# Masked scores of two heads in one bank: TensorE adds the mask, VectorE takes both minima at once, ScalarE exponentiates from PSUM

## What is computed

```python
def blk(i):                       # forgetting_attention, one block of 128 queries
    mask = pos[None, :] <= tq[:, None]
    s = jnp.einsum('bqhd,bshd->bhqs', qb, kf) + cq[..., None] - c[:, :, None, :]
    p = jax.nn.softmax(jnp.where(mask, s, -jnp.inf), axis=-1)
    return jnp.einsum('bhqs,bshd->bqhd', p, vf)
```

## Time and profile before

| | |
|---|---|
| median of 3 runs | 1352.73 us (1351.6 to 1353.11) |
| profiled execution | 1355.96 us, span 1354.3 us |
| TensorE busy, mean granted clock | 1330.4 us (98%), 0.993 |
| VectorE busy | 641.7 us (47%) |
| ScalarE busy | 243.1 us (18%) |
| units 16 to 47 with what is between (a0) | 107.69 to 150.92 us |
| units 48 to 79 with what is between (a1) | 460.38 to 497.84 us |

### The profile page before, as it was taken

The page is one execution under the profiler, slowest core; times in us unless marked ns, Lnnn a source line. Parts: engine busy times, 40 slices in busy tenths (PEclk is TensorE's granted clock), DMA queues, the critical chain, the costliest instruction groups (busy, mean ns, idle before and its releaser), DMA issues.

```text
span 1354.3 us, 18984 instructions
## 1 busy us (share of the span) xinstructions
PE 1330.4 (98%) x7306; PEld 823.3 (61%) x7306; DVE 641.7 (47%) x1224; ACT 243.1 (18%) x573; POOL 89.1 (7%) x114
## 2 busy tenths in 40 slices
PE   9999999999999999999999999999999999999996
PEld 8677575786747856586686675744444444444433
DVE  1226589877862257977979263421221222212213
ACT  2135311211102450120123162100000000000002
POOL 1116500000000120000000100000000000000001
PEclk9997999999999999999999999999999999999999
DMA  9931154565453414676574405399999999999994
GB/s 381 354 109 65 64 205 178 219 237 216 183 197 150 157 45 190 236 292 263 221 276 168 158 34 216 147 421 419 421 421 413 422 421 421 422 420 421 421 421 195
DMA packets 51006, 359.53 MB, mean 265 GB/s; under 512 B 5888, under 2 KB 6096, under 8 KB 8432
## 3 DMA queue, kind: packets, MB, share of 16 engines
q1 hardware_dynamic: 45248, 324.60, 59.5%
q0 software_dynamic: 5392, 32.05, 6.6%
q10 hardware_dynamic: 288, 1.80, 0.3%
HBM read 356.88 MB, written 1.05 MB: 264 GB/s over the span
## 4 chain that ended last, share of the span: by engine, by line
PE 82%; DVE 7%; issue 1%; ACT 1%; DVEq 0%; ACTq 0%
PE ps L1470 13%; PE ps L980 13%; PE ps L971 11%; PE ps L1499 7%; PE ps L1395 7%; PE ps L1448 7%; PE ps L953 5%; PE ps L794 4%; PE ps L799 2%; PE ps L873 2%; PE ps L892 1%; PE ps L831 1%; PE ps L1355 1%; PE ps L1224 1%; PE ps L1241 1%
## 5 line engine op out<-in xcount | busy, mean ns | idle before, releaser
L2698 DVE TENSOR_TENSOR masked_and_probs<-ps,gate_rows 128x512 f32<-128x512 f32 x52 | 33.5, 686 | 152.4 <-PE ps L1499 152.4
L794 PE MATMUL ps<-xT,ring 128*128 128x256 f32 x432 | 94.7, 380 | 0.8 <-DVE xT L1992 0.8
L1448 PE MATMUL ps<-masked_and_probs,probT 128*128 128x512 f32 x208 | 94.4, 594 | 1.0 <-DVE masked_and_probs L2698 1.0
L1395 PE MATMUL ps<-masked_and_probs,mix_rows 128*128 128x256 f32 (+1 forms) x416 | 93.0, 376 | 0.0
L1395 PEld LDWEIGHTS ps<-masked_and_probs,mix_rows 128*128 128x128 f32 x416 | 75.0, 190 | 28.8 <-issue 19.6
L971 PEld LDWEIGHTS ps<-xT,ring 128*128 128x128 f32 x768 | 87.8, 192 | 3.8 <-issue 3.8
L1607 ACT ACTIVATE qk_tiles<-ps 64x256 f32<-64x256 f32 (+3 forms) x84 | 39.2, 468 | 278.0 <-PE ps L971 241.8
L794 PEld LDWEIGHTS ps<-xT,ring 128*128 128x128 f32 x432 | 81.5, 190 | 12.3 <-ACT xT L1595 1.0
L971 PE MATMUL ps<-xT,ring 128*128 128x128 f32 x768 | 88.7, 275 | 0.0
L980 PE MATMUL ps<-ring,qk_tiles 128*128 128x512 f32 x192 | 85.2, 592 | 0.0
L953 PE MATMUL ps<-ring,xT 128*128 128x512 f32 x192 | 83.8, 593 | 0.0
(11 more groups left out here) (469 smaller groups left out, 2260.8 us busy)
## 6 DMA issues: line engine op xcount, KB each, us to landing
ring<-in_stream SPq DMA_DIRECT2D x200, 1024.0 KB, 8.6
qk_tiles<-in_stream SPq DMA_DIRECT2D x46, 1024.0 KB, 20.3
v_rows<-in_ada POOLq DMA_DIRECT2D x12, 1024.0 KB, 5.1
qk_tiles<-in_ada POOLq DMA_DIRECT2D x12, 1024.0 KB, 5.2
vec_rows<-in_stream SPq DMA_DIRECT2D x12, 1024.0 KB, 17.2
con<-in_stream SPq DMA_DIRECT2D x12, 1024.0 KB, 18.2
y_rows<-in_stream SPq DMA_DIRECT2D x12, 1024.0 KB, 19.7
par<-in_stream SPq DMA_DIRECT2D x12, 1024.0 KB, 20.8
```

The costliest lines, as they stand in the source:

```text
L794: mm = pe.matmul(ps[0:n, bank, off:off + T], w[:, kk, col:col + n], src[:, k, :], start=bank not in started, stop=k == KT - 1, skip_group_ ...
L1395: mm = pe.matmul(ps[:, 5 + kk // 2, kk % 2 * 2 * P:kk % 2 * 2 * P + width], h2[:, t, k * P:(k + 1) * P], select[:, t, 0:width], start=t == ...
L1448: mm = pe.matmul(ps[:, q, :], probT[:, buf, 256 + q // 2 * P:256 + (q // 2 + 1) * P], yslot[:, q % 2 * 512:(q % 2 + 1) * 512], start=False ...
L2698: dve.tensor_tensor(yslot[:, cols], ps[:, 5 + half, :], gaterow[:, 1, cols], ALU.mult).then_inc(ready, 1)
```

## The change

In units 16 to 79 (`PAIRED`) two heads go through the stages together.

- TensorE writes the scores of both into one bank, side by side, and after each adds the mask on the diagonal block of 128 keys: the product of the identity and `hidden`, which is the negated causal mask, accumulated onto the scores (L899 and L902 of the kernel after, in `masked_scores`). Scale and sign have moved into ScalarE's copies of keys and queries.
- VectorE takes the minima of both heads with one TENSOR_REDUCE from PSUM (L2239) and copies both transposed heads with one COPY (L2264). `masked` is no longer written.
- ScalarE's exponentials read the bank. It copies no transposed heads in a1 any more, and makes `hidden` once (128x128).
- The scores of a pair wait for the exponentials of an earlier pair (`s_exp`) and no longer for `s_mask`: up to unit 35 for the pair two before, then for the pair four before.
- The transposes of a pair come at step i-4, the values at i-6, in a0 and a1.
- In the second kind the order of heads is 0, 2, 1, 3, 4, 6, 5, 7, so that both heads of a pair lie in the same 64 partitions. `sum_column` keeps the columns of `esum` in the old order.
- Units 34 and 35 still use two banks (`TWO_BANKS`), and a0 has one step more.

```diff
+PAIRED = range(16, 80)
-            for h in range(8):
+            for h in (0, 2, 1, 3, 4, 6, 5, 7):
-TWO_BANKS = 34
+TWO_BANKS = 36
 def by_scalar(u):
-    return u % 4 == 1 and (UNITS[u][0] == "loc" or ...)
+    return u % 4 == 1 and u not in PAIRED and (UNITS[u][0] == "loc" or ...)
+        hidden = causal[:, 0, P:2 * P]
+        def pair_scores(u):
+            p, nk = u // 2, UNITS[u][3]
+            bank = p % 2 if u < TWO_BANKS else (0, 1, 6, 7)[p % 4]
+            return ps[:, bank, 0:2 * nk].rearrange("p (n k) -> p n k", n=2)
...
+            def wait_scores_read(u):
+                if u < INSTANCES["a0"][1]:
+                    if u == PAIRED[0]:
+                        pe.wait_ge(s_mask, u)
+                    elif u > PAIRED[0] + 2:
+                        pe.wait_ge(s_exp, u - 2 if u < TWO_BANKS else u - 6)
+                elif u >= INSTANCES["a1"][0] + 8:
+                    pe.wait_ge(s_exp, u - 6)
+            def masked_scores(u, pair):
+                def mask(n):
+                    qt, nk = UNITS[u + n][1], UNITS[u + n][3]
+                    return pe.matmul(scores(u + n)[:, qt * P:nk], ident, hidden, start=False, stop=True, skip_group_check=True)
+                for n, (lhs, keys) in enumerate(pair):
+                    pe.matmul(scores(u + n), lhs, keys[0][0], start=True, stop=False, skip_group_check=True)
+                    mm = mask(n)
+                mm.then_inc(s_sc, 2)
+            def turn_pair(u):
+                pe.wait_ge(s_exp, u + 2)
+                if u == PAIRED[0] and u < INSTANCES["a1"][0]:
+                    pe.wait_ge(s_pTsb, u - 1)
+                elif u >= PAIRED[0] + 2:
+                    pe.wait_ge(s_pTsb, u - 2)
+                for n in range(2):
+                    for t in range(UNITS[u][3] // P):
+                        mm = pe.transpose(turned_bank(u + n)[:, t * P:(t + 1) * P], prob[:, (u + n) % 4, t * P:(t + 1) * P], ident)
+                mm.then_inc(s_pT, 2)
...
+                    u = i - 4
+                    if a <= u < b and u in PAIRED and u % 2 == 0:
+                        turn_pair(u)
...
+                    u = i - 6
+                    if name == "a0" and a <= u < b and u in PAIRED and u % 2 == 0:
+                        row_sums(u)
+                        row_sums(u + 1)
...
-                        act.activation(prob[:, u % 4, 0:nk], masked[:, u % 4, 0:nk], ACT.Exp, bias=negmax[:, u:u + 1],
-                                       scale=-1.0, accum_out=esum[:, u:u + 1]).then_inc(s_exp, 1)
+                        act.activation(prob[:, u % 4, 0:nk], scores(u) if u in PAIRED else masked[:, u % 4, 0:nk], ACT.Exp, bias=negmax[:, u:u + 1],
+                                       scale=-1.0, accum_out=esum[:, sum_column(u):sum_column(u) + 1]).then_inc(s_exp, 1)
+            copy(hidden, causal[:, 0, 0:P], scale=-1.0)
-            copy(kvraw[:, 0, :], ps[:, 1, 0:T])
+            copy(kvraw[:, 0, :], ps[:, 1, 0:T], scale=-SCALE)
...
+                    if i < b and i in PAIRED and i % 2 == 0:
+                        dve.wait_ge(s_sc, i + 2)
+                        dve.tensor_reduce(negmax[:, i:i + 2], pair_scores(i), AX, ALU.min).then_inc(s_mask, 2)
...
+                    u = i - 4
+                    if a <= u < b and u in PAIRED and u % 2 == 0:
+                        dve.wait_ge(s_pT, u + 2)
+                        dve.tensor_copy(pair_probs(u), pair_turned(u)).then_inc(s_pTsb, 2)
```

More of the change, by code:

```diff
@@ L236, with sum_column @@
 ROPE_AT = (12, 16)
+PAIRED = range(16, 80)
 def by_scalar(u):
-    return u % 4 == 1 and (UNITS[u][0] == "loc" or UNITS[u][0] == "fox" and UNITS[u][1] == 1)
+    return u % 4 == 1 and u not in PAIRED and (UNITS[u][0] == "loc" or UNITS[u][0] == "fox" and UNITS[u][1] == 1)
 def taken_before(u, scalar):
     return sum(by_scalar(w) == scalar for w in range(u + 1))
+def sum_column(u):
+    kind, _, h, _, _, _, g = UNITS[u]
+    first = group_units(g)[0]
+    return first + h - UNITS[first][2] if kind in ("slc", "win") else u
 def group_units(g):
@@ L597, in factors, with pair_probs @@
             return mix[:, 1, 0:512]
+        def pair_probs(u):
+            if u < INSTANCES["a1"][0]:
+                buf = probT[:, u // 2 % 2, :]
+            else:
+                buf = (probT[:, 0, :], probT[:, 1, :], mix[:, 0, 0:512], mix[:, 0, 512:1024])[u // 2 % 4]
+            return buf[:, 0:2 * UNITS[u][3]]
         def turned_probs(u):
+            if u in PAIRED:
+                return pair_probs(u)[:, u % 2 * UNITS[u][3]:(u % 2 + 1) * UNITS[u][3]]
             if u < INSTANCES["a1"][0]:
@@ L843, in turn_factors, with row_sums @@
                 mm.then_inc(s_fT, 1)
+            def wait_scores_read(u):
[24 more added lines that the diff above has]
+                mm.then_inc(s_pT, 2)
+            def row_sums(u):
+                _, _, _, vals = unit_operands(u)
+                _, _, _, nk, col, w, g = UNITS[u]
+                wait_probs(u)
+                if u == group_units(g)[0] and g >= 2:
+                    pe.wait_ge(s_odone, g - 1)
+                for t, val in enumerate(vals):
+                    n = min(P, nk - t * P)
+                    mm = pe.matmul(ps[:, 4 + g % 2, col:col + w], turned_probs(u)[0:n, t * P:(t + 1) * P], val,
+                                   start=t == 0, stop=t == len(vals) - 1)
+                if u == group_units(g)[-1]:
+                    mm.then_inc(s_o, 1)
             def attention(name, pieces=None):
                 a, b = INSTANCES[name]
-                for i in range(a, b + (4 if name == "a0" else 5)):
+                for i in range(a, b + 5):
                     if i < b and i % 2 == 0:
@@ L864, in attention @@
                             pe.wait_ge(s_projsb, 12)
-                        if i >= 2:
+                        if i in PAIRED:
+                            wait_scores_read(i)
+                        elif i >= 2:
                             pe.wait_ge(s_mask, i if i < TWO_BANKS + 2 else i - 2)
                         pair = [unit_operands(i + n)[:2] for n in range(2)]
-                        for k in range(len(pair[0][1])):
+                        if i in PAIRED:
+                            masked_scores(i, pair)
+                        for k in range(len(pair[0][1]) if i not in PAIRED else 0):
                             for n, (lhs, keys) in enumerate(pair):
@@ L897, in attention @@
                     u = i - 4
[L898 to L910, removed]
+                    if name == "a0" and a <= u < b and u not in PAIRED:
+                        row_sums(u)
+                    u = i - 6
+                    if name == "a0" and a <= u < b and u in PAIRED and u % 2 == 0:
+                        row_sums(u)
+                        row_sums(u + 1)
                     for piece in (pieces or {}).get(i - a, ()):
@@ L2142, in attention @@
                 a, b = INSTANCES[name]
-                for i in range(a, b + (6 if name == "a0" else 7)):
-                    if i < b:
+                for i in range(a, b + 7):
+                    if i < b and i in PAIRED and i % 2 == 0:
+                        dve.wait_ge(s_sc, i + 2)
+                        dve.tensor_reduce(negmax[:, i:i + 2], pair_scores(i), AX, ALU.min).then_inc(s_mask, 2)
+                    if i < b and i not in PAIRED:
                         kind, qt, h, nk, _, _, _ = UNITS[i]
```

30 lines of the change are left out of this document (20 added, 10 removed).

## The result

| | before | after |
|---|---|---|
| median (lowest to highest), 6 executions each | 1352.92 us (1351.6 to 1354.46) | 1384.6 us (1372.04 to 1405.26) |
| profiled execution, span | 1355.96, 1354.3 us | 1373.09, 1371.3 us |
| second-kind stage (a0), profiled | 43.2 us | 53.3 us |
| odd stage (a1), profiled | 37.5 us | 44.2 us |

The change made the kernel slower: ratio 1.019, 95% interval 1.0141 to 1.0238. I had predicted 1356.9 us in a range of 1352.5 to 1364.5; the result lies far outside. The executions after fall on three levels, two each: 1372 to 1373 us at a mean granted clock of 0.998, 1384.5 at 0.988 and 1405 at 0.973. The ratio leaves out executions more than 1.5% above the fastest, so it speaks of the lower levels, and the median of the table lies above it.

A forecast was written before the change was run, and what follows sets the result against it. TensorE, busy for 98% of the span, was taken as the bound. Stage a0 at -1.2 us and a1 at +5.4 gave +4.2, put on the median 1352.7: 1356.9 us, range 1352.5 to 1364.5.

The forecast's parts named there:

- What TensorE gains in work: Both stages: 64 masks at 0.225 us plus pairs losing their two array halves, 10.0 us in a0, 7.2 in a1.
- Forecast 42.0 us for the stage: a0 after the change: 40.8 us of work plus 1.2 of waits, against 43.2 before, so -1.2 us.
- where I had said 6: a0: about 6 us of waits for `s_mask` and single units' short latency would pay part of the new work.
- the 5 us that I put on the fall: a0: about 5 us lost to the lower clock before, counted as paying part of the 10 us of new work.
- rival 1: a0: the clock still falls for 14.6 us, adding 7.3 us; total +11.5, 1364.2 us; chance 0.18.
- A denser stage keeps the clock: a0: the first query tile's fuller steps hold the clock at 1.00; this was the main forecast, chance 0.60.
- Forecast +5.4: a1: 34.1 us of work, 7.2 of masks and 1.6 of waits kept make 42.9, against 37.5 before.
- The tail wait: End of a1: without scores between transposes and values, the copy of 0.68 us stands open once or twice.
- Rival 3: Both stages: pairing lengthens the pipeline, 0.12 us for each of 32 pairs, +4 us on top, 1361; chance 0.07.
- Rival 2: Both stages: a mask takes only 0.12 us, 64 cost 7.7 instead of 14.4; total -2.5, 1350.2; chance 0.08.
- Rival 4: Both stages: all waits vanish, leaving 40.8 + 41.3 against 80.7, +1.4 us, 1354.1; chance 0.07.
- That no other stage would move: Rest of the kernel: the two stages' end shifts pass one to one to the program's end; later stages stay unchanged.

The follow-up runs named there:

- whole_rows: The change with second-kind keys zero-padded so scores work on 128 partitions, against the kernel before: 1360.91 us, ratio 1.0057.
- switch_probe: Kernel before with seven series of products on 64, 66 and 128 partitions, in a row or alternated, put in front: 1402.56 us, one execution.
- second_alone: The change in units 16 to 47 only, units 48 to 79 as in the kernel before: 1379.04 us, ratio 1.018.
- after_again: The changed kernel itself, unaltered, run on another chip: 1404.44 us, ratio 1.0376 against the kernel before.
- masks_last: The changed kernel with both scores of a pair first, then both masks, 32 partition changes fewer: 1366.59 us, ratio 1.0083 against the kernel before.
- no_masks: The changed kernel without the mask products in units 16 to 79, so it computes other values: 1399.73 us, ratio 1.032 against the kernel before.
- lag_only: Kernel before with only the change's pairwise transposes, copies and values at later steps; scores, masks, minima as before: 1359.22 us, ratio 1.0038.
- whole_rows_second: The change for the second kind alone, with keys zero-padded to 128 partitions, odd layer as before: 1355.5 us, ratio 1.0006.
- before_whole: Kernel before with nothing changed but second-kind keys zero-padded to 128 partitions: 1352.4 us, ratio 0.9991.

## Why the prediction was wrong

**The step that failed** is the price of scores and masks in a0, under "What TensorE gains in work". I priced the mask from products between neighbours of its own kind and the scores from the odd layer, as if the neighbour did not matter. In a0 each pair now goes between 64 and 128 partitions four times. Forecast 42.0 us for the stage, measured 53.3; with the changes taken out and all else kept, whole_rows measured 41.7. The step's other terms were thus right: the mask at 0.22, the pair of 256 keys in turn at some 0.9. That the sum comes so near is in part luck: of whole_rows' 41.7 us TensorE is busy for 41.3 and idle for 0.4, where I had 40.8 of work and 1.2 of waits.

**Reading.** Behind that stands a reading that two numbers could satisfy. A pair with 256 keys took 0.63 before and I concluded that its halves overlap only in part. It was 0.43 for two halves side by side plus 0.19 for one change; the other change that a pair pays shows in the distances of its neighbours. The Trainium skill ("TensorE: Matmul & The Clock Gate", Part 3) says that matmuls in distinct row groups run concurrently; I wrote that the trace doesn't agree, and the probe shows that it does, with records of both halves starting together. The Trainium skill ("TensorEngine Tiling (Array Packing)", Key Properties) also says that changing the tiling mode drains TensorE; I did not weigh it, and the probe agrees with a cost of 0.19 us a change, none for 66 partitions.

**The a0 stage, once more, at full clock.** No profile of before holds the clock there. From the executions at 0.998, before is 1351.6 and after 1372.5, 20.9 apart, of which a1 has 6.8, so a0 lost some 14 us and was about 39 us long before. An estimate with the probe's prices: masks 7.2; 64 changes instead of 32, 6.1; halves in turn, 8 x 0.43 + 8 x 0.22 = 5.2; together 18.5. Some 4.5 us of it came back in waits, where I had said 6.

**The clock.** Two errors. First, I took the 5 us that I put on the fall in the profiled execution as recovered, and then put the sum on the median, 3.2 us lower, where the fall mostly is not: the same us counted in part twice. (The low stretch was also read too long: 0.79 in 129 to 132 puts its end at 130.3 and not at 131.4, and 0.84 over 43.23 us makes it 13.8 us and not 14.6.) Second, rival 1 (the clock still falls, 0.18) was right in kind and far too small. The low stretch is not 14.6 us but about 27 (second_alone) or 67 (after_again, 84.42 us at a mean of 0.60), and half of that gives the levels of 1384.5 and 1405. "A denser stage keeps the clock" fell: TensorE was busy for 9.75 of 10 us when after_again lost it, and for all of 115 to 120 us in second_alone. The Trainium skill ("TensorE: Matmul & The Clock Gate", Part 1) has the fall after an idle window; here it came while the profile shows TensorE busy. Shown is that it depends on the partitions of the scores. How is open. It may be the share of the array that works, or the changes: masks_last, with 32 changes and 64-partition scores, kept the clock in this stage, and no_masks, with as many changes and less work, lost it in all four executions, but on another chip. And in all seven profiles in which the clock fell in this stage, it fell soon behind the sixteen 30-column products of the compressed part (115.61 to 117.41 us in second_alone, the fall near 118.3). These stand in the kernels that kept the clock too, and no run takes them out, so their part, which the prediction suspected, stays untested.

**The odd stage.** Forecast +5.4, measured +6.8. A mask costs the 0.22 us that I said, and no change of partitions is paid, since 66 are as 128; but no_masks shows that the 32 masks of 7.2 us stand for only 4.7 us of the stage. The tail wait was foreseen in kind ("stands open once or twice" at 0.68) and mis-sized: 2.4 us, where I kept 1.6 for all waits. Rival 3 (the longer pipeline, 0.07) is real here: lag_only alone loses 2.9 us.

**The rest.** Rival 2 is refuted, since a mask takes 0.22 at best. Rival 4 too, since both stages end above their floors. That no other stage would move held to 0.2 us.

## What to carry to other kernels

Before a small product is put between others on TensorE, look at the partitions of its neighbours: a mask of 0.22 us cost about twice that between scores on 64 partitions, and nothing extra between scores on 66 or on zero-padded 128. Where the trace shows two products overlapping by a part only, test whether it is full overlap plus a fixed price at its ends. And where executions fall on levels of the clock, make the sum for one level and compare it with executions of that level alone. A variant that computes other values may do other work elsewhere: look at the stages that it should not touch.

## What the runs showed of the hardware

- A change between 64 and 128 partitions costs TensorE 0.19 us in both directions (0.415 for 0.23 at 128 columns, 0.63 for 0.43 at 256), without a trace of idle time. Between 66 and 128 it costs nothing.
- The granted clock can fall to 1.2 GHz while TensorE shows no idle time, and stay there for 27 (second_alone) or 67 us (after_again) of busy records. The change's own kernel did so in all four executions of after_again and in four of the six of the result, at 12 or 33 us above its lowest level. With the scores on 128 partitions (whole_rows, whole_rows_second, before_whole) the mean clock of the execution was 0.996 or more in all 29.
- Two products on the lower and the upper 64 partitions run side by side: 0.22 us for both at 128 columns, half of the time in turn (switch_probe).
